# Three rearrangements in the first layer of a fused transformer kernel: a shift matrix through device memory, state matrices on another queue, half units in other places

## The chip, the cores and the metric

The kernel runs on one core of one Trainium2 chip. The metric is the device time of one execution in microseconds (us); lower is better. Engines are called by the names of the profile: PE (TensorE matmul), PEld (its weight loads), DVE (VectorE), ACT (ScalarE), POOL (GpSimd) and SP (SyncE, which issues most transfers). An engine with a q behind it (SPq, ACTq) is the instruction queue that issues DMAs.

## The reference, cut to what matters

Everything is float32, with batch 1, 256 positions and width 1024. The program is one even layer, a feed-forward network, one odd layer, a feed-forward network, and then a second block (feed-forward, mixer, cross attention to a memory, feed-forward, final norm). The change lies in the even layer alone:

```
hn = rmsnorm(x, even_norm)
q, k, v, u = split(hn @ even_w_in, [512, 640, 768])     # 8 query heads, 2 key heads, u has 512 channels
q, k = rmsnorm(q, q_norm), rmsnorm(k, k_norm)            # by head
o_attn = swa_sink_attention(q, k, v, sinks)              # window 128
o_ssm  = s5_mixer(u, a, b, c, d, log_dt, w_glu, b_glu)   # 32 groups, 64 complex states, 16 channels
x = x + concat(o_attn, o_ssm) @ even_w_out
hn = rmsnorm(x, ffn_norm); x = x + (silu(hn @ w_gate) * (hn @ w_up)) @ w_down
```

The state-space mixer `s5_mixer` is a linear recurrence in 64 complex states for each of 32 groups of 16 channels. The kernel computes it in chunks of S = 8 positions: inside a chunk as a product with a block-triangular matrix, and between chunks as a scan over 32 chunk states.

## The kernel before, in words

**Units.** Weights arrive from device memory in units of 1 MB in a ring of three buffers `raw`. SP issues each load (`load`, L563) when the unit that had the buffer is used up (`w_used`). In the even layer units u0 to u0+4 are the five 256-column parts of `even_w_in`: u0 and u0+1 give u transposed (`whole_t`, L712, 16 products each, all in float32), u0+2 to u0+4 give q, k and v (`whole_n`, L724, which can be done in two halves, one for each 128 rows). Unit u0+5 is the gate matrix (L1161), u0+6 and u0+7 multiply the gated mixer output (`out_glu`, L1181), u0+8 and u0+9 the attention output (`out_heads`, L694, split in high and low parts, which ACT makes at L1632 and DVE at L2172). The next unit belongs to the cross attention's memory (`mem_k1`), and then the first feed-forward network begins.

**PE's order** is written out by hand in `even()` (L957). It is: flips (transposes) of the state matrices' raw form `a_raw`; the flips of the normed input, `norm(0)` (L805, the line of all flips); 64 small flips that bring B and C from `bc_nat` into PSUM; u0; u0+1; flips of u into chunks; u0+2; again such flips; flips of the chunked u and of V (`v_in`); the 32 chunk-state products (L1021); the first half of u0+3; the flips of these states, straight and with halves swapped (L805, L1037); the lag products K (L1050), which need B and C scaled by powers (`bb_ready`, `wc_ready`, from a long row of DVE operations that ends at L2483); the second half of u0+3 and the first of u0+4; two products with `jt`; the second half of u0+4; flips of q; `convolve(0)`, the flips of the keys, `convolve(1)` (L1086, L1089); the attention scores (`window_scores`, L1121 to L1130); flips of y; the gate; the output units, with `probs` and `values_t` between them; `out_heads(0)`, `norm(8)` (the flips of the normed memory), `out_heads(1)`.

**The shift.** The lag products K end in SBUF as `lags`: 64 rows (16 channels of each of 4 group columns), 8 lags, 8 groups, 16 channels. For `convolve` they must stand as a block Toeplitz matrix `m_in`, in which the block rows j = 0 to 7 hold the first j+1 lags, shifted. 32 DMAs from SBUF to SBUF do this, one for each j and group column, 18 of them issued by SP and 14 by ACT:

```
for j, cc in M_SP:
    sp.dma_start(m_in[PC * j:PC * j + PC, cc, S - 1 - j:, :, :],
                 lags[32 * cc:32 * cc + PC, 0:j + 1, :, :]).then_inc(m_in_done, 16)
sp.wait_ge(m_in_done, 16 * 4 * S)
```

ACT issues its share (L1847) between its copies `qkv_out(1)` and `qkv_out(2)` (L1808, L1811); the latter empties unit u0+4 for the norm of q and k (squares on ACT L1851, a sum on DVE L2511, a root on POOL L1583 to L1585, the product on DVE L2518). POOL adds the skip term to lag 0 first (L1578).

**Start.** SP issues x, three small loads for a and dt (`ssm_loads`, L551), the constants, the gain, two loads of B and four of C (`bc_loads`, L620), and then u0 to u0+2 and 19 small vectors (L624). ACT has no load of its own there.

**The end of the layer.** DVE takes the softmax rows in a fixed order: `front` (maximum, L2536 to L2540) and `back` (division, L2376 to L2378) for six tiles, and `gated` (L2549), the product that `out_glu` waits for. After `norm(8)` ACT makes the high parts (L1693) and DVE the low parts (L2217) of the normed memory, then DVE adds the layer's output to x (L2341).

## Time and profile before

| what | value |
|---|---|
| median of 3 runs | 1213.48 us (1212.47 to 1213.51) |
| the profiled execution: its time / its span | 1212.6 us / 1210.9 us |
| PE busy in the span | 1182.2 us (98%) |
| DVE / ACT / POOL busy | 782.9 / 588.2 / 64.9 us |
| bytes moved | 206.05 MB, mean 170 GB/s |
| even layer: start of the first unit / of the scores / of `out_glu` | 16.84 / 84.09 / 98.03 us |
| start of the unit `mem_k1`, behind the even layer's last unit | 131.98 us |

The span runs from the first to the last instruction of the profile; times inside it are counted from its start. "Idle before, releaser" is what ended an engine's wait. A line number is one of the kernel before. One product of float32 operands is two records of PE, a flip is one record.

### The profile page before, as it was taken

The numbers are of one execution on the slowest core, as the hardware profiler recorded it, in microseconds if no ns is written. First come the engines' busy times: TensorE is split into PE (matmuls) and PEld (weight loads), VectorE is DVE, ScalarE is ACT, GpSimd is POOL, SyncE is SP. The second block draws the span as 40 slices with busy tenths as digits, with TensorE's granted clock in tenths as the row PEclk, the third lists the DMA queues.
The fourth block names the chain that finished last, engine by engine and source line by source line (L and its number), as shares of the span: only waits on it lengthen the run. The fifth ranks groups of instructions, "written<-read, shape, count | busy, mean of one in ns | idle before, by whom it ended". The sixth has DMA issues, their size and how long they took to land.

```text
span 1210.9 us, 17637 instructions
## 1 busy us (share of the span) xinstructions
PE 1182.2 (98%) x7043; PEld 1021.8 (84%) x7043; DVE 782.9 (65%) x845; ACT 588.2 (49%) x729; POOL 64.9 (5%) x81
## 2 busy tenths in 40 slices
PE   6989999999999999999999999999999999999997
PEld 5866888888899988888888888888889988888886
DVE  6956666666755557666667666667594646766665
ACT  5446644444566655434445444345574545444443
POOL 2110000000002110000000000000011000000000
PEclk9999999999999999999999999999999999999999
DMA  8254565565544346555655656555533534656561
GB/s 208 88 144 135 165 189 194 182 199 182 184 156 150 130 153 195 189 194 183 198 179 171 201 180 207 176 199 174 182 128 117 181 132 131 199 183 199 180 201 70
DMA packets 158120, 206.05 MB, mean 170 GB/s; under 512 B 9833, under 2 KB 131249, under 8 KB 158065
## 3 DMA queue, kind: packets, MB, share of 16 engines
q1 hardware_dynamic: 157616, 204.51, 52.6%
q10 hardware_dynamic: 448, 0.77, 0.4%
q8 instruction: 39, 0.64, 0.2%
q14 instruction: 17, 0.13, 0.0%
HBM read 203.04 MB, written 1.05 MB: 169 GB/s over the span
## 4 chain that ended last, share of the span: by engine, by line
PE 90%; DVE 5%; ACT 2%; DMA 1%; ACTq 1%; issue 1%; SPq 1%; POOL 0%; POOLq 0%; DVEq 0%
PE outp L753 26%; PE acc L694 20%; PE outp L694 19%; PE outp L757 13%; PE acc L805 2%; PE outp L712 1%; PE outp L724 1%; PE outp L1181 1%; DVE w_lo L2172 1%; DVE h_pair L2217 1%; PE outp L859 1%; DMA raw<-in_even_w_in_dram 1%; ACTq L1847 1%; ACT w_hi L1632 0%; ACT h_pair L1693 0%
## 5 line engine op out<-in xcount | busy, mean ns | idle before, releaser
L1632 ACT ACTIVATE w_hi<-raw 128x2048 fp32r<-128x2048 f32 x177 | 339.5, 1918 | 411.5 <-PE outp L757 283.7
L2172 DVE TENSOR_TENSOR w_lo<-raw,w_hi 128x2048 fp32r<-128x2048 f32 x177 | 405.4, 2290 | 177.5 <-ACT w_hi L1632 177.4
L753 PE MATMUL outp<-h_pair,w_hi 128*128 128x512 f32 x1056 | 253.8, 391 | 0.3
L753 PEld LDWEIGHTS outp<-h_pair,w_hi 128*128 128x128 f32 x1056 | 195.0, 188 | 42.6 <-DVE h_pair L2217 4.2
L757 PEld LDWEIGHTS outp<-h_pair,w_lo 128*128 128x128 f32 x1056 | 135.4, 191 | 5.1
L694 PE MATMUL acc<-w_hi,f_lo 128*128 128x512 f32 x352 | 137.4, 390 | 0.0
L694 PE MATMUL acc<-w_hi,f_hi 128*128 128x512 f32 x352 | 137.4, 390 | 0.0
L694 PE MATMUL acc<-w_lo,f_hi 128*128 128x512 f32 x352 | 137.0, 389 | 0.0
L757 PE MATMUL outp<-h_pair,w_lo 128*128 128x256 f32 x1056 | 137.0, 283 | 0.0
L694 PE MATMUL outp<-w_hi,h_pair 128*128 128x512 f32 (+1 forms) x416 | 114.0, 361 | 0.5 <-DVE w_lo L2172 0.3
L2271 DVE TENSOR_REDUCE arena<-outp 128x256 f32<-128x512 f32 x88 | 56.7, 687 | 58.4 <-PE outp L757 56.1
L2284 DVE TENSOR_REDUCE arena<-outp 128x256 f32<-128x512 f32 x88 | 56.7, 687 | 56.3 <-PE outp L757 56.1
L694 PEld LDWEIGHTS outp<-w_hi,h_pair 128*128 128x128 f32 x416 | 73.0, 189 | 13.8 <-issue 1.6
L694 PEld LDWEIGHTS acc<-w_lo,f_hi 128*128 128x128 f32 x352 | 66.1, 188 | 14.0
L694 PEld LDWEIGHTS acc<-w_hi,f_hi 128*128 128x128 f32 x352 | 66.2, 188 | 12.6
L753 PE MATMUL outp<-m_pair,w_hi 128*128 128x512 f32 x320 | 76.7, 392 | 0.0
L694 PEld LDWEIGHTS acc<-w_hi,f_lo 128*128 128x128 f32 x352 | 66.2, 188 | 12.3
L694 PE MATMUL outp<-w_lo,h_pair 128*128 128x512 f32 (+1 forms) x208 | 74.2, 357 | 0.0
L694 PE MATMUL outp<-h_pair,w_hi 128*128 128x256 f32 x384 | 70.8, 286 | 0.0
L753 PEld LDWEIGHTS outp<-m_pair,w_hi 128*128 128x128 f32 x320 | 59.3, 188 | 12.5 <-issue 0.2
L694 PEld LDWEIGHTS outp<-h_pair,w_hi 128*128 128x128 f32 x384 | 59.8, 191 | 0.9 <-issue 0.5
L1553 POOL TENSOR_SCALAR arena<-arena 128x1 f32<-128x1 f32 x20 | 9.7, 487 | 911.0 <-ACT xn L1655 887.4
(334 smaller groups left out, 1427.0 us busy)
## 6 DMA issues: line engine op xcount, KB each, us to landing
raw<-in_ffn_w_gate_dram SPq DMA_DIRECT2D x44, 1024.0 KB, 5.6
raw<-in_ffn_w_up_dram SPq DMA_DIRECT2D x44, 1024.0 KB, 5.5
raw<-in_ffn_w_down_dram SPq DMA_DIRECT2D x44, 1024.0 KB, 4.9
raw<-in_odd_w_in_dram SPq DMA_DIRECT2D x12, 1024.0 KB, 5.2
raw<-in_w_in_dram SPq DMA_DIRECT2D x10, 1024.0 KB, 5.2
raw<-in_even_w_in_dram SPq DMA_DIRECT2D x5, 1024.0 KB, 9.1
raw<-in_even_w_out_dram SPq DMA_DIRECT2D x4, 1024.0 KB, 6.9
raw<-in_cross_wk_dram SPq DMA_DIRECT2D x4, 1024.0 KB, 5.7
```

Source lines behind the costliest of these rows:

```text
L694: ins = nc.tensor.matmul(dst, lhs, rhs, start=start and n == 0, stop=stop_ and n == 2, skip_group_check=skip)
L712: ins = nc.tensor.matmul(outp[:, k % NB, m * L:(m + 1) * L], w[:, c, m * P:(m + 1) * P], h_f32[:, c, :], start=c == 0, stop=c == C - 1)
L724: ins = nc.tensor.matmul(outp[:, k % NB, t * UW:(t + 1) * UW], h_f32[:, c, t * P:(t + 1) * P], w[:, c, :], start=c == 0, stop=c == C - 1)
L753: nc.tensor.matmul(bank, w[0][:, c, m * P:(m + 1) * P], x[:, :, c, :], start=c == 0, stop=c == C - 1, skip_group_check=True)
L757: ins = nc.tensor.matmul(outp[:, (k + m) % NB, 0:L], w[1][:, c, m * P:(m + 1) * P], x[:, 0, c, :], start=False, stop=c == C - 1, skip_grou ...
L805: return nc.tensor.transpose(dst, src, ident[base:base + rows, base:base + rows])
L859: nc.tensor.matmul(outp[:, (k + m) % NB, :].rearrange("p (a l) -> p a l", l=L)[:, :, rows], w[:, c, m * P:(m + 1) * P], m_pair[:, :, c, ro ...
L1181: ins = nc.tensor.matmul(outp[:, (ko + 2 * j + t) % NB, :], sig[:, c, t * P:(t + 1) * P], w[:, c, :], start=c == 0, stop=False, skip_group ...
L1632: A(w_hi[:, slot(u), :], raw[:, u % RAW, :], ACT.Copy).then_inc(w_hi_ready, 1)
L2172: tt(w_lo[:, slot(u), :], raw[:, u % RAW, :], w_hi[:, slot(u), :].bitcast(F32), ALU.subtract).then_inc(w_lo_ready, 1)
L2271: V.reduce_sum(silu[:, j % 2, m * L:(m + 1) * L], bank.rearrange("p (a l) -> p l a", l=L), AX).then_inc(out_free[(k + m) % NB], 1)
L2284: V.reduce_sum(b[:, m * L:(m + 1) * L], bank.rearrange("p (a l) -> p l a", l=L), AX).then_inc(out_free[(k + m) % NB], 1)
```

## The change

Five edits, all in the even layer:

1. The three loads for a and dt, the two of B and the loads of C go from SP's queue to the front of ACT's. C is loaded in its natural order in two loads instead of four.
2. The flips of B (32) stay ahead of u0; those of C go between u0 and u0+1, as 64 products with the identity, 32 rows by 64 columns each, since C's halves are now made by writing the product twice, to partitions 0 to 63 and 64 to 127. DVE waits for the first, ACT for both before its copies L1788.
3. The first half of u0+3 moves from behind the chunk-state products to ahead of the flips of the chunked u; the second half moves from behind the lag products K to ahead of them.
4. The shift goes through a device-memory tensor `lag_rows`: four DMAs write the lags (two by SP, two by ACT), both queues wait for all four, and eight DMAs (one for each j, all group columns together) read them into `m_in`, four on each queue. SP then loads u0+6 and u0+7 ahead of the memory `mem_sb`. ACT's `qkv_out(1)` comes before its copies of the lags.
5. PE does `convolve(1)` right after `convolve(0)`, then the flips of the keys, then those of y, then the scores. ACT loads its table for the gelu before it copies the keys. DVE does `gated(0)` ahead of the first two divisions. `norm(8)` stands ahead of `out_heads(0)`.

```diff
+        b_loads = [(bc_nat[G * j:G * j + G, :].rearrange("g (h m) -> g h m", h=2),
+                    a[n][0].rearrange("g n p -> g (n p)").unsqueeze(1).to_broadcast([G, 2, 1024]))
+                    for j, n in enumerate(["ssm_b_re", "ssm_b_im"])]
-        bc_loads += [(bc_nat[G * j + 64:G * j + 64 + G, :].rearrange("g (p h n) -> g p h n", h=2, n=N)[:, :, h, :],
-                      a[n][0]) for j, n in enumerate(["ssm_c_re", "ssm_c_im"]) for h in range(2)]
+        c_loads = [(bc_nat[G * j + 64:G * j + 64 + G, 0:N * PC], a[n][0].rearrange("g p n -> g (p n)"))
+                   for j, n in enumerate(["ssm_c_re", "ssm_c_im"])]
+        lag_rows = nc.dram_tensor("lag_rows", (4 * PC, S * 8 * PC), F32, kind="Internal").ap()
+        def lags_out(eng, cc):
+            eng.dma_start(lag_rows[PC * cc:PC * cc + PC, :],
+                          lags[32 * cc:32 * cc + PC, :, :, :].rearrange("p s i c -> p (s i c)")).then_inc(lag_out, 16)
+        def lags_in(eng, j):
+            eng.dma_start(m_in[PC * j:PC * j + PC, :, S - 1 - j:, :, :].rearrange("p a s i c -> p a (s i c)"),
+                          lag_rows.rearrange("(a p) m -> p a m", p=PC)[:, :, 0:(j + 1) * 8 * PC]).then_inc(m_in_done, 16)
...
@@ SP @@
-                for j, cc in M_SP:
-                    sp.dma_start(m_in[PC * j:PC * j + PC, cc, S - 1 - j:, :, :],
-                                 lags[32 * cc:32 * cc + PC, 0:j + 1, :, :]).then_inc(m_in_done, 16)
-                sp.wait_ge(m_in_done, 16 * 4 * S)
+                for cc in range(2):
+                    lags_out(sp, cc)
+                sp.wait_ge(lag_out, 16 * 4)
+                for j in (7, 5, 3, 1):
+                    lags_in(sp, j)
+                sp.wait_ge(m_in_done, 16 * S)
+                for j in range(2):
+                    load(u0 + 6 + j, quarter(w_out, 1, j), 512)
                 sp.dma_start(mem_sb, a["mem_2"][0].rearrange("(t p) f -> p t f", p=P)).then_inc(mem_in, 16)
...
@@ PE @@
+                pe.wait_ge(b_in, 16 * 2)
                 for p in range(PC):
-                    for j in range(4):
...
+                    for j in range(2):
+                        ins = flip(outp[:, (OUT["even_b"] + j) % NB, p * G:(p + 1) * G],
+                                   bc_nat[G * j:G * j + G, p::PC], G, G * j)
                 ins.then_inc(bc_flipped, 1)
+                whole_t(u0, OUT["even_u0"], fresh=chunks(0))
+                pe.wait_ge(c_in, 16 * 2)
...
+                for p in range(PC):
+                    for h in range(2):
+                        for j in range(2):
+                            rows = slice(G * (j + 2), G * (j + 3))
+                            ins = nc.tensor.matmul(outp[N * h:N * h + N, (OUT["even_c"] + j) % NB, p * G:(p + 1) * G],
+                                                   bc_nat[rows, p * N:(p + 1) * N], ident[rows, rows],
+                                                   start=True, stop=True)
+                ins.then_inc(bc_flipped, 1)
+                whole_t(u0 + 1, OUT["even_u1"])
...
                 u_chunked(1)
+                whole_n(u0 + 3, k0 + 3, (0,))
...
-                whole_n(u0 + 3, k0 + 3, (0,))
                 emptied(pe, ACC["st"], 2)
...
+                whole_n(u0 + 3, k0 + 3, (1,))
                 pe.wait_ge(bb_ready, 2)
                 pe.wait_ge(wc_ready, 1)
...
-                whole_n(u0 + 3, k0 + 3, (1,))
                 whole_n(u0 + 4, k0 + 4, (0,))
...
                 convolve(0)
-                (flips of the keys)
                 convolve(1)
-                (window_scores(0), then the flips of y)
+                (flips of the keys, the flips of y, then window_scores(0))
...
+                norm(8)
                 out_heads(0, True)
-                norm(8)
                 out_heads(1)
...
@@ ACT @@
+                (the loads ssm_loads, b_loads, c_loads ahead of everything)
+                qkv_out(1)
                 (copies of the lags)
-                qkv_out(1)
-                for j, cc in M_ACT: (14 DMAs)
+                for cc in (2, 3):
+                    lags_out(nc.scalar, cc)
+                act.wait_ge(lag_out, 16 * 4)
+                for j in (6, 4, 2, 0):
+                    lags_in(nc.scalar, j)
                 qkv_out(2)
...
-                qk_out(ACC["kt"], k_t, L, 1)
                 y_out(1)
                 nc.scalar.preload_act_table_set("gelu_apprx_tanh_and_others")
+                qk_out(ACC["kt"], k_t, L, 1)
...
@@ DVE @@
+                gated(0)
                 back(0)
                 back(1)
-                gated(0)
-                back(2)
                 gated(1)
```

Lines in round brackets stand for lines that are only moved.

## Rows read from the trace of the kernel before

**Rows 1.** The page: the span, and the chain that ended last by engine.

```profile
span 1210.9 us, 17637 instructions
...
PE 90%; DVE 5%; ACT 2%; DMA 1%; ACTq 1%; issue 1%; SPq 1%; POOL 0%; POOLq 0%; DVEq 0%
```

**Rows 2.** Windows by stage: length, busy PE, PEld, DVE, ACT, POOL, clock, DMA.

```profile
33.31:61.18 27.87, 24.56 (x248) 22.02 (x247) 27.32 (x17) 13.75 (x27) 2.14 (x2) 1.00 0.24 77
61.18:84.09 22.91, 19.73 (x255) 16.14 (x255) 11.97 (x13) 5.99 (x10) 5.31 (x4) 1.00 0.47 117
```

**Rows 3.** The chain, 0 to 35: start, duration, what.

```profile
7.38 9.07 DMA raw<-in_even_w_in_dram
...
16.84 16.47 PE outp L712 x64
```

**Rows 4.** Timeline 0 to 20: start, duration, operation, idle before and its releaser.

```profile
6.08 0.63 ACT L1655 ACTIVATE xn<-x_sb 128x512 f32<-128x512 f32 x1 [4.00 <-DMA x_sb<-in_x_dram]
...
9.40 3.87 PE L805 MATMUL acc<-arena,xn 128*128 128x128 f32 x16 [1.30 <-DVE xn L2206]
...
13.62 1.97 PE L805 MATMUL outp<-arena 32*128 32x32 f32 x64 [0.35 <-DMA arena<-in_ssm_c_im_dram]
```

**Rows 5.** Window of one microsecond, columns as in rows 2.

```profile
3.00:4.00 1.00, 0.00 (x0) 0.00 (x0) 0.00 (x0) 0.00 (x0) 1.00 (x1) 1.00 0.97 401
```

**Rows 6.** Windows of the products L712 alone: length, PE, PEld, clock, DMA share, GB/s.

```profile
17.00:21.20 4.20, 4.20 (x10) 3.35 (x11) 1.00 1.11 351
22.00:26.20 4.20, 4.20 (x21) 3.71 (x20) 1.00 0.31 38
```

**Rows 7.** Groups by form, 44 to 64: busy us, mean ns, idle before.

```profile
L805 PE MATMUL acc<-arena 32*128 32x32 f32 x32 | 2.1, 221 | 1.1 <-ACT arena L1800 1.1
...
L1037 PE MATMUL acc<-arena 128*64 128x128 f32 x32 | 2.0, 276 | 0.0
```

**Rows 8.** Timeline 53 to 64, columns as in rows 4.

```profile
53.87 0.60 ACT L1953 ACTIVATE arena<-acc 128x512 f32<-128x512 f32 x1 [0.27 <-PE acc L1021]
...
61.18 2.06 PE L1050 MATMUL acc<-arena 128*16 128x128 f32 x64 [0.95 <-issue]
```

**Rows 9.** The shift's issues by SP: ns of one, first and last start.

```profile
L632 SPq DMA_DIRECT2D arena_end<-arena x18: 589/596/763, 65.2 to 76.3; - x18
```

**Rows 10.** DMA issues: size of one, median us from issue to landing.

```profile
arena_end<-arena ACTq DMA_DIRECT2D x4, 64.0 KB, 2.7
...
out_dram<-xn SPq DMA_DIRECT2D x2, 512.0 KB, 2.7
```

**Rows 11.** Window of the shift, columns as in rows 2.

```profile
70.00:80.00 10.00, 7.88 (x78) 5.92 (x80) 4.17 (x5) 3.03 (x4) 0.32 (x2) 1.00 0.60 103
```

**Rows 12.** Timeline 60 to 120, columns as in rows 4.

```profile
75.99 0.60 ACT L1811 ACTIVATE arena<-outp 128x512 f32<-128x512 f32 x1 [8.40 <-PE outp L724]
...
78.71 0.43 PE L1086 MATMUL acc<-arena_end,arena 128*32 128x128 f32 x8 [0.79 <-DMA arena_end<-arena]
...
84.81 1.28 ACT L1870 ACT_TABLE_LOAD   x1
...
98.03 2.38 PE L1181 MATMUL outp<-raw,arena 128*128 128x512 f32 x5 [0.98 <-DVE arena L2549]
...
118.05 0.69 DVE L2382 TENSOR_TENSOR h_pair<-acc,h_pair 128x512 fp32r<-128x512 f32 x1 [0.61 <-ACT h_pair L1958]
```

**Rows 13.** The chain, 60 to 90.

```profile
63.24 3.67 PE outp L724 x16
...
81.76 0.41 PE acc L805 x2
...
84.09 0.67 PE outp L1121 x2
```

**Rows 14.** The chain, 95 to 140.

```profile
117.59 5.70 PE outp L694 x24
...
129.72 2.20 DVE w_lo L2172
```

More of the change, by code:

```diff
@@ L138, in build @@
                  if (what == "half" and i % 2 == 0) or (what == "values" and i < 6)]
-    OUT = plan([("even_bc", 4), ("even", 5), ("even_sc", 4), ("even_out", 4), ("mem_k1", 1), ("ffn0", 44), ("mem_k0", 1), ("odd", len(ODD_BANKS)),
+    OUT = plan([("even_b", 2), ("even_u0", 1), ("even_c", 2), ("even_u1", 1), ("even", 3), ("even_sc", 4), ("even_out", 4), ("mem_k1", 1), ("ffn0", 44), ("mem_k0", 1), ("odd", len(ODD_BANKS)),
                 ("odd_out", 4), ("mem_k2", 1), ("ffn1", 44), ("mem_k3", 1), ("ffn2", 44), ("mem_v0", 1), ("mix", 10),
@@ L548, in _ @@
             sp.dma_start(x_sb[:, :, :], a["x"][0].rearrange("(t p) f -> p t f", p=P)).then_inc(x_loaded, 16)
-            if "even" in running:
-                for dst, src in ssm_loads:
-                    sp.dma_start(dst, src).then_inc(ssm_in, 16)
             sp.dma_start(early, a["consts"][:, 0:EARLY_W]).then_inc(consts_in, 16)
@@ L618, in _ @@
                 w = by_p(a["even_w_in"][0])
-                for dst, src in bc_loads:
-                    sp.dma_start(dst, src).then_inc(bc_in, 16)
                 for j, n in enumerate([3, 4, 0]):
@@ L957, in even @@
             def even():
-                u0, k0 = UNITS["even"], OUT["even"]
+                u0, k0 = UNITS["even"], OUT["even"] - 2
                 pe.wait_ge(consts_in, 16)
@@ L1092, in even @@
                 convolve(0)
-                k = ACC["kt"]
-                acc_taken(pe, k)
-                pe.wait_ge(qk_ready, 1)
-                for t in range(T):
-                    ins = flip(acc[:, k % NB, t * P:(t + 1) * P], qkv[:, t, 512:640])
-                ins.then_inc(acc_ready, 1)
                 convolve(1)
@@ L1133, in window_scores @@
                                 ins.then_inc(sc_ready if i < 2 else acc_ready, 1)
-                emptied(pe, ACC["qk"], 2)
-                emptied(pe, ACC["kt"])
-                pe.wait_ge(mask_ready, 1)
-                window_scores(0)
+                k = ACC["kt"]
+                acc_taken(pe, k)
+                pe.wait_ge(qk_ready, 1)
+                for t in range(T):
+                    ins = flip(acc[:, k % NB, t * P:(t + 1) * P], qkv[:, t, 512:640])
+                ins.then_inc(acc_ready, 1)
                 for j in range(2):
@@ L1763, in even @@
             def even():
-                u0, k0 = UNITS["even"], OUT["even"]
+                u0, k0 = UNITS["even"], OUT["even"] - 2
+                for dst, src in ssm_loads:
+                    nc.scalar.dma_start(dst, src).then_inc(ssm_in, 16)
+                for dst, src in b_loads:
+                    nc.scalar.dma_start(dst, src).then_inc(b_in, 16)
+                for dst, src in c_loads:
+                    nc.scalar.dma_start(dst, src).then_inc(c_in, 16)
                 act.wait_ge(x_loaded, 16)
@@ L1784, in even @@
                 A(small[:, 15, :], turns[:, 1, :], ACT.Sin, scale=TWO_PI).then_inc(lam_sin, 1)
-                act.wait_ge(bc_flipped, 1)
-                for j, part in ((2, cr), (3, ci)):
-                    k = OUT["even_bc"] + j
+                act.wait_ge(bc_flipped, 2)
+                for j, part in ((0, cr), (1, ci)):
+                    k = OUT["even_c"] + j
                     A(part.rearrange("p g c -> p c g"), outp[:, k % NB, :].rearrange("p (c g) -> p c g", g=G),
@@ L1842, in even @@
                       ACT.Copy).then_inc(acc_free[k % NB], 1)
-                qkv_out(1)
                 act.wait_ge(kz_ready, 1)
                 act.wait_ge(k_ready, 1)
-                for j, cc in M_ACT:
-                    nc.scalar.dma_start(m_in[PC * j:PC * j + PC, cc, S - 1 - j:, :, :],
-                                        lags[32 * cc:32 * cc + PC, 0:j + 1, :, :]).then_inc(m_in_done, 16)
+                for cc in (2, 3):
[3 more added lines that the diff above has]
+                    lags_in(nc.scalar, j)
                 qkv_out(2)
@@ L2398, in even @@
             def even():
-                u0, k0 = UNITS["even"], OUT["even"]
+                u0, k0 = UNITS["even"], OUT["even"] - 2
                 dve.wait_ge(x_loaded, 16)
@@ L2556, in even @@
                     front(nth)
+                gated(0)
                 back(0)
                 back(1)
-                gated(0)
-                back(2)
                 gated(1)
-                for nth in range(3, 6):
+                for nth in range(2, 6):
                     back(nth)
```

43 lines of the change are left out of this document (20 added, 23 removed), and 2 rows, old and new, of the table ACC.

## The prediction

> **What bounds the kernel now.** I read the page first, for its chain: PE carries 90% of what ended last, in a span of 1210.9 us [rows 1]. So outside the even layer nothing is to be had here, and a microsecond saved on PE's way through the layer is kept. Then the windows by stage, to see where PE is not full. Between 33.31 and 61.18 PE is busy 24.56 of 27.87 us and DVE 27.32: there DVE's row of operations for B and C (it ends with `wc_ready`) runs beside PE without a pause, and both arrive at the lag products K together, PE with 0.95 us of waiting [rows 2, 8]. Between 61.18 and 84.09 PE is busy 19.73 of 22.91 us [rows 2]. Then the chain and the timeline of the start: x lands at 6.08, PE flips x until 13.27, does 64 small flips from 13.62 to 15.59, and begins u0 at 16.84, when its weights, asked for at 7.38, have landed after 9.07 us [rows 3, 4]. Last the shift: SP alone issues 18 DMAs at 0.6 us each from 65.2 on, `convolve(0)` starts at 78.71 behind them, and ACT comes to `qkv_out(2)` only at 75.99, behind its own 14 issues [rows 9, 12].
>
> **Start.** Seven loads on ACT at about 0.5 us each cost ACT 3.5 us, inside the 4.00 us that it waits for x anyway [rows 4]. SP asks for u0 after three loads instead of twelve, some 5 us earlier, so its wait of 9.07 us ends long before PE is free; that wait goes. What is late next is PE itself. x used to have the DMA engines to itself at 401 GB/s [rows 5]; now 512 KB of B are under way beside its second half. Between 0 (they start too late to matter) and 512 KB / 401 GB/s = 1.3 us, plus 0.3 for the small ones: x lands 0 to 1.6 us later; I take 0.8, the middle. This moves all that hangs on x. The Trainium skill (DMA: Bandwidth & Descriptors, "Issuing engines are not separate DMA queues") says that the two queues share the same 16 engines and take turns, which speaks against the edit: by it nearly all of B's bytes would go ahead of x's end, the 1.6 us end; by the row of 401 GB/s and a late start, the 0.
>
> The flips of B are 32 of 64. The 64 ran at 0.031 us, taking turns over four groups of 32 partitions [rows 4]; 32 flips from one group took 2.1 us, 0.065 each [rows 7]. With two groups the price lies between 32 x 0.031 = 1.0 and the full 2.0; I take 1.5. So u0 starts at 13.27 + 0.8 + 1.5 + 0.1 = 15.7, **1.15 us earlier**.
>
> In u0 PE makes 10 records in 4.2 us, later 21 in as long, though the granted clock reads 1.00 in both windows [rows 6]: half and full pace, 1.2 and 2.4 GHz. It is slow from 16.84 until about 21.6, which costs 2.4 us. The sum keeps this loss; ends 0 and -2.4.
>
> **C between u0 and u0+1.** 64 float32 products are 128 records. Nearest rows: 0.031 us per flip when all groups take turns, and 2.0 / 32 = 0.062 per record for the products with the identity L1037, which alternate between two column halves as these do but move 128 columns, not 32 [rows 4, 7]. So 3.9 us, or 7.9; below, half of 3.9, if they pair up over rows and columns, is 2.0. I take 3.5: the columns are few, so what is left is the pace of issue. Half of the old 64 flips was C's, but it lay ahead of u0 and is counted there. **+3.5.** ACT's copies of B and C's parts have time until DVE needs them at 44.
>
> **The halves of u0+3.** Ahead of the chunked flips the first half covers ACT's copies, for which PE waited 1.1 us [rows 7]: -1.1. It no longer covers the copies of the chunk states (0.60 us; the last begins at 53.87, with the half [rows 8], and the handovers add 0.3): +0.9. The second half, ahead of K, takes the wait for `wc_ready`: -0.95 [rows 8]. PE ends u0+4 at 75.5 - 1.15 + 3.5 - 1.15 = 76.7, 1.2 late. But K is late by that and by the half of 3.65 us: it ends at 63.24 + 4.85 = 68.1 [rows 8, 13], and the lags, with ACT's copy and POOL's addition (63.24 to 65.2 before), are ready at 70.0 instead of 65.2.
>
> **The shift.** Out: two issues per queue; the last, issued 0.6 later, lands after 2.15 (64 KB within SBUF took 2.7, 512 KB into device memory also 2.7, of which 512 KB / 401 GB/s = 1.3 is the bytes' own time: 1.6 to 2.7 for 64 KB, the middle taken [rows 5, 10]): 2.75. The Trainium skill (DMA: Bandwidth & Descriptors, "Anatomy of one DMA") puts most of a transfer's fixed 2 us to the receipt of the write and calls device memory the heaviest target; the store row shows no such surcharge, and the sum has none. Back in: four issues of 0.64 on each queue, the last landing 2.7 behind its start: 4.6 at least; 1.18 MB at 300 GB/s takes 3.9 and starts 1.4 behind the first issue: 5.25. The old shift moved 103 GB/s at a share of 0.60 [rows 11], or 172 at full share: 6.9 + 1.4 = 8.3 at most. So `m_in` is whole at 70.0 + 2.75 + 5.25 = **78.0** (77.3 to 81.1), against 78.7 [rows 12]. The 13.5 us of the old shift shrink to 8.0, and 4.85 of the 5.5 gained are spent ahead of it. ACT leaves its queue at about 75.3, ahead of u0+4's end at 76.7; nobody waits there. The DMA traffic that u0+6 and u0+7 now precede (`mem_sb`, needed at 102) costs nothing.
>
> **To the scores.** Two convolutions of 1.9 (82.17 to 84.09 was one [rows 13]) end at 81.9. Behind them ACT copies y1 (0.6), loads its table (1.28 [rows 12]), copies the keys (0.5), with three handovers of 0.15: scores at **84.7**. By the other way, u0+4's end at 76.7 plus 5.8 (75.99 to 81.6, and 0.2) has the keys normed at 82.5, in time. So +0.6 against 84.09 [rows 13]. Flips of y and scores change places; DVE's two `front` rows decide the gate's start either way, 5.7 us behind.
>
> **The end.** PE waited 0.98 us for `gated(0)` at 98.03 [rows 12]; behind the last `front` instead of behind two divisions it is done 2 us earlier: **-0.98**. `norm(8)` ahead of `out_heads(0)`: its last bank is free only when DVE has made the low parts, at 118.74 [rows 12], so PE ends it at 120.1 and starts the heads 2.5 us later than at 117.59; without the 1.9 us of flips between them, both take 2 x 5.7 [rows 14] and end at 131.2 instead of 130.5. But the memory's parts and DVE's split, behind which `mem_k1` began at 131.98 [rows 14], are now early: it starts at 131.2, -0.8, and 0.15 more for the row flips behind it. **-0.95.**
>
> **Sum.** +0.6 - 0.98 - 0.95 = -1.3 us. The profiled execution took 1212.6 for its span of 1210.9, and stands 0.9 below the median of 1213.48. 1212.6 - 1.3 = 1211.3 by its own time, **1212.2** by the median. Less than 0.2% (2.43 us) is about what a measurement of this kernel cannot tell from no change.
>
> **Rivals.**
> - *Faster, by the clock.* PE's pause of 1.25 us ahead of u0 goes [rows 4]. If full pace comes at u0's start instead of 4.8 us into it, 2.4 us go with it, and since PE bounds everything up to the scores all of it arrives: 1209.8. For it: PE is now busy without a break from 10 on. Against: it was busy from 9.40 to 15.59 too, with a break of 0.35, and began u0 slow. The Trainium skill (TensorE: Matmul & The Clock Gate, Part 1) says that sustained busyness raises the clock; by it a part or all of the 2.4 us could go.
> - *Slower, by C's products.* At 0.062 us a record they take 7.9 instead of 3.5: K, the shift and the scores slip by 4.4, to 1216.6. It decides beyond 3.5 + 3.7 = 7.2 us. Against: a quarter of the columns.
> - *The shift is no faster than before.* At 8.3 us for the way in, the scores start 3.1 later: 1215.3, slower.
> - *x is on time and the small prices are at their low ends:* -0.8 for x, -0.5 for B, up to -1.5 for C: 1209.4.
>
> **Chances.** The forecast, with its neighbours within 0.2%: 0.48; its own range is 1211.1 to 1214.5. Clock 0.26 and low ends 0.10: faster 0.36. C's products 0.08, the shift 0.08: slower 0.16. The range leaves a tenth on each side: below, it takes in the clock's and the low ends' times, 1209.2; above, the late shift, 1215.4.
>
> **What the profile will show.** u0 (L712 of before) at 15.7 and without a DMA as releaser; 128 records of C in 3.5 us; K's end near 68; the lag DMAs from 70.0, `m_in` read at 78; no wait ahead of `out_glu` and of `mem_k1`. I am wrong if x lands at 7.7 or on time, if u0 takes under 8.5 us (it took 9.5), if C takes over 5, if K ends outside 66 to 70, or if the way in lasts over 7 us.

## The result: slower by 0.26%, and the profile after

The changed kernel takes 1216.52 us (median of 19 runs, 1214.39 to 1219.92) against 1213.48 (19 runs): ratio 1.0026, 95% interval 1.002 to 1.0032. The forecast was 1212.2 with a range that ended at 1215.4. It is outside, on the other side.

The profiled execution of the changed kernel took 1219.92 us, the longest of its 19. Its stages show where time goes, but not in the amounts of the median, so sizes are read below from medians of experiments too.

The page: the span, and the chain by engine, beside [rows 1].

```profile
span 1218.2 us, 17808 instructions
...
PE 92%; DVE 3%; DMA 2%; ACT 2%; issue 0%; ACTq 0%; SPq 0%; POOL 0%; POOLq 0%
```

The timeline of PE and ACT in the first 30 us, beside [rows 4]; below it the piece of the chain that stands where [rows 3] had 9.07 us of the same transfer.

```profile
6.25 0.63 ACT L1672 ACTIVATE xn<-x_sb 128x512 f32<-128x512 f32 x1 [0.25 <-DMA x_sb<-in_x_dram]
...
13.06 1.95 PE L813 MATMUL outp<-arena 32*128 32x32 f32 x32
15.72 8.86 PE L720 MATMUL outp<-h_whole,raw 128*128 128x256 f32 x32 [0.71 <-DMA raw<-in_even_w_in_dram]
24.51 2.07 PE L989 MATMUL outp<-arena 32*64 32x32 f32 x128
26.50 7.17 PE L720 MATMUL outp<-h_whole,raw 128*128 128x256 f32 x32
```

```profile
2.27 13.41 DMA raw<-in_even_w_in_dram
```

u0 begins at 15.72, as forecast, but not for the forecast's reason: PE waits 0.71 us for the weights, whose load takes 13.41 us instead of 9.07, with x, B and C under way beside it, and lands only at 15.67. C's products take 2.07 us. PE ends u0+1 at 33.68 in the chain, 0.37 behind the 33.31 of [rows 2].

The timeline of PE and ACT's queue in the middle of the layer, beside [rows 8, 12]:

```profile
54.59 1.95 PE L1040 MATMUL acc<-arena 128*32 128x128 f32 x64 [1.30 <-ACT arena L1978]
...
60.18 3.72 PE L732 MATMUL outp<-raw,h_whole 128*128 128x256 f32 x16
63.83 2.02 PE L1069 MATMUL acc<-arena 128*16 128x128 f32 x64
...
67.39 0.84 ACTq L516 DMA_DIRECT2D lag_rows<-arena  x2
71.26 1.80 ACTq L521 DMA_DIRECT2D arena_end<-lag_rows  x4
...
74.51 1.04 PE L813 MATMUL acc<-arena 128*128 128x128 f32 x8
82.03 0.65 PE L1104 MATMUL acc<-arena_end,arena 128*32 128x128 f32 x8 [6.48 <-DMA arena_end<-lag_rows]
...
91.06 1.00 PE L813 MATMUL acc<-arena 32*128 32x32 f32 x29 [1.49 <-ACT arena L1881]
91.99 1.22 PE L1133 MATMUL outp<-h_pair 128*128 128x512 f32 x2
```

K ends at 65.9 instead of 63.24 (the moved half unit stands at 60.18 ahead of it), the lags leave at 67.39 instead of 65.2, the way out takes 3.85 us and the way in 10.7 (14.6 together, where the old shift took 13.5), and PE stands idle for 6.48 us ahead of `convolve`, where it had waited 0.79 [rows 12]. Eight products of `convolve` take 0.65 us instead of 0.43. The scores start at 91.99 (92.06 by the chain) instead of 84.09 [rows 13], and the feed-forward network's start is late with them. The DMA issues of the way in (size, median us to landing), beside [rows 10]:

```profile
arena_end<-lag_rows SPq DMA_DIRECT2D x1, 256.0 KB, 5.1
arena_end<-lag_rows ACTq DMA_DIRECT2D x1, 224.0 KB, 6.2
...
arena_end<-lag_rows ACTq DMA_DIRECT2D x1, 32.0 KB, 9.4
```

Windows, columns as in [rows 2] (the last three are the clock, the DMA share and GB/s), beside [rows 11]:

```profile
76.00:77.00 1.00, 0.00 (x0) 0.00 (x0) 0.27 (x1) 1.00 (x2) 0.00 (x0) 1.00 1.05 132
...
81.00:82.00 1.00, 0.00 (x0) 0.00 (x0) 0.00 (x0) 0.00 (x0) 1.00 (x1) 0.50 0.00 0
82.00:84.00 2.00, 1.97 (x40) 1.82 (x44) 0.00 (x0) 0.00 (x0) 0.60 (x1) 0.50 0.48 32
...
94.00:98.00 4.00, 4.00 (x22) 2.61 (x20) 2.44 (x9) 2.47 (x8) 0.00 (x0) 0.50 0.00 0
```

Two things are to be seen. During the way in the DMA engines are near a full share but move little: 132 GB/s in this window, and over the whole way in 1.18 MB for a summed share of 8.9 us, which is 133 GB/s at a full share (x had 401 [rows 5]). And the granted clock is 0.50 (1.2 instead of 2.4 GHz) from 81 to 87, from within PE's idle 6.48 us on, and again from 92 to 98, behind the wait that ends at 91.06.

The end is as planned. In the chain `out_glu` follows the gate without a wait, and the memory's unit the heads:

```profile
99.98 7.12 PE acc L1178 x32
107.10 6.87 PE outp L1198 x16
...
129.01 13.76 PE outp L702 x72
142.77 0.90 PE acc L813 x8
```

From `out_glu` to the row flips behind `mem_k1` it is 142.77 - 107.10 = 35.67 us. Before, it was 135.24 - 98.03 = 37.21 (this row of its chain was not shown; [rows 12] for the other):

```profile
135.24 1.16 PE acc L805 x8
```

### The profile page after: what moved, and what is told of

Read it like the earlier page. It is cut to its first block, busy times and chain, and to the rows that moved or that the text cites. A ratio compares the mean times of both kernels' runs of the same rounds, so it can differ in the third digit from the quotient of the medians.

```text
span 1218.2 us, 17808 instructions
## 1 busy us (share of the span) xinstructions
PE 1188.4 (98%) x7139; PEld 1027.7 (84%) x7139; DVE 783.2 (64%) x845; ACT 588.2 (48%) x729; POOL 64.6 (5%) x81
## 3 DMA queue, kind: packets, MB, share of 16 engines
q10 hardware_dynamic: 944, 1.49, 0.6%
## 4 chain that ended last, share of the span: by engine, by line
PE 92%; DVE 3%; DMA 2%; ACT 2%; issue 0%; ACTq 0%; SPq 0%; POOL 0%; POOLq 0%
PE outp L761 26%; PE outp L702 20%; PE acc L702 20%; PE outp L765 13%; PE acc L813 2%; PE outp L720 1%; PE outp L732 1%; PE outp L1198 1%; DMA raw<-in_even_w_in_dram 1%; DVE w_lo L2197 1%; DVE h_pair L2242 1%; DMA arena_end<-lag_rows 1%; PE outp L867 1%; PE acc L1178 1%; ACT w_hi L1649 0%; ACT h_pair L1710 0%
## 5 line engine op out<-in xcount | busy, mean ns | idle before, releaser
L702 PEld LDWEIGHTS outp<-w_hi,h_pair 128*128 128x128 f32 x416 | 73.1, 189 | 13.4 <-DVE w_lo L2197 1.3
## 6 DMA issues: line engine op xcount, KB each, us to landing
raw<-in_even_w_in_dram SPq DMA_DIRECT2D x5, 1024.0 KB, 13.4
```

Of the source, the lines that this page charges most:

```text
L702: ins = nc.tensor.matmul(dst, lhs, rhs, start=start and n == 0, stop=stop_ and n == 2, skip_group_check=skip)
```

## The experiments

All ratios are against the kernel before, run on the same chip. Where two experiments are compared by their medians, they may come from two chips, on which the kernel before had 1213.1 to 1213.9 (1212.8 in a single run). "Start", "shift", "halves", "end" are the edits 1 and 2, 4, 3, and 5 without its reordering of keys and flips of y.

### Parts undone in the changed kernel

**The half unit and ACT's copy behind.** The changed kernel with the second half of u0+3 behind K, and `qkv_out(1)` behind ACT's lag transfers.

```diff
-                whole_n(u0 + 3, k0 + 3, (1,))
                 pe.wait_ge(bb_ready, 2)
...
+                whole_n(u0 + 3, k0 + 3, (1,))
                 whole_n(u0 + 4, k0 + 4, (0,))
...
-                qkv_out(1)
...
                     lags_in(nc.scalar, j)
+                qkv_out(1)
                 qkv_out(2)
```

> The changed kernel with one thing put back: the second half of u0+3 stands behind the lag products K again, and ACT's copy of that unit behind its lag DMAs. Theory A (the late K and a slow way in together leave PE idle, and the idle time also costs clock): K ends near 62.7 instead of 65.9, the lags go out at 64, m_in is whole near 79, PE idles about 3 us instead of 6.5 ahead of convolve, the granted clock stays 1.00 there; 3 to 6 us faster than the changed kernel, about 1211 to 1213. Theory B (only the way in counts, K's place does not): m_in near 82 still, no gain.

Measured: 1212.68 us, 0.999 (0.9982 to 0.9999): 3.8 below the changed kernel. Its timeline of PE, and a window:

```profile
61.05 2.04 PE L1068 MATMUL acc<-arena 128*16 128x128 f32 x64 [1.30 <-issue]
...
76.87 0.43 PE L1104 MATMUL acc<-arena_end,arena 128*32 128x128 f32 x8 [0.63 <-DMA arena_end<-lag_rows]
```

```profile
84.00:88.00 4.00, 4.00 (x25) 2.79 (x20) 0.61 (x1) 3.32 (x5) 0.00 (x0) 0.50 0.65 256
```

PE waits 1.30 us ahead of K and only 0.63 ahead of `convolve`, which starts 5.2 us earlier at the full clock. The second stretch at half clock stays. ACT's copy, which was put back too, is not the cause by the trace of the changed kernel: there it ran from 63.94 to 64.6, and ACT then waited for the lag products (0.40 and 0.32 us), so the lags were not late by it. What is left is the half unit. It filled a pause of PE with work and delayed the transfer that everything waits for.

Not all of the 5.2 us is shown to be its effect. The lags leave 2.3 us earlier (65.08); the way out is 1.0 us shorter here (2.8) and the way in 1.8 (8.9), with the same transfers. In the other runs with unchanged rows the way in was 9.9 to 11.4 us; why it was short here is not shown.

**The old shift.** The changed kernel with the 32 transfers within SBUF in the place of the twelve.

> The changed kernel with the old shift (32 DMAs within SBUF, 18 by SP, 14 by ACT), all other edits kept. Theory A: issued from 67.3 on at 0.6 us each, m_in is whole near 80.8, 1.2 us earlier than through device memory, PE still idles 5 us and the clock still falls: within 2 us of the changed kernel, 1214.5 to 1216.5. Rival (the way through device memory is the whole loss): back to 1212 or below.

Measured: 1217.7 us (6 runs), 1.0036 (1.0024 to 1.0048). This is above both expectations, and by the intervals no different from the changed kernel (1.0026). PE waits 5.3 us, `convolve` starts at 78.8, at half clock. That is 3.2 us earlier than in the changed kernel's profile, but most of it arises at the start: in this execution the 32 products of u0 took 7.17 us instead of 8.86, the pace of the full clock from the first one on, and K ends at 63.8 instead of 65.9. From K's end to `convolve` the old shift takes 15.0 us and the new one 16.1, so that the 1.2 us of the expectation are there, and the clock falls behind it as before.

**Spare products in the wait.** Six products with `jt` that nobody reads, ahead of PE's wait for `m_in`.

```diff
+                acc_taken(pe, ACC["y0"])
+                for _ in range(6):
+                    nc.tensor.matmul(acc[:, ACC["y0"] % NB, :], jt,
+                                     g_st[:, 0:16, :].rearrange("p g c -> p (g c)"), start=True, stop=True)
                 pe.wait_ge(m_in_done, 16 * S)
```

> The changed kernel with six more products of 128x512 on PE while it waits for m_in, into the bank that convolve(0) then overwrites; nothing else differs. Theory A (the idle time costs clock, not only itself): m_in still whole near 82, but the granted clock stays 1.00 behind it, convolve takes 3.9 us instead of 6.5, and the scores and the gate run at full pace: 1 to 5 us faster than the changed kernel. Rival (the clock has nothing to do with the idle time, or the slow stretch falls elsewhere): no gain, and a granted clock near 0.5 at 82 to 88 as before.

Measured: 1214.49 us (11 runs), 1.0011 (1.0002 to 1.0019): 2.0 below the changed kernel. Its timeline:

```profile
74.81 5.32 PE L1094 MATMUL acc<-arena 128*128 128x512 f32 x12
81.52 0.42 PE L1108 MATMUL acc<-arena_end,arena 128*32 128x128 f32 x8 [1.40 <-DMA arena_end<-lag_rows]
```

`m_in` is no earlier, PE only works more, and the kernel is faster: eight products take 0.42 us again and the clock reads 1.00 in every window from 76 to 98. So the clock's fall was about 2 us of the median (1.8 by the ratios, whose intervals just do not meet).

### Parts done alone in the kernel before

**The shift alone.**

> The kernel before with the new shift alone (four DMAs out, eight in, PE and all other orders as before). Lags ready at 65.2, but ACT's two writes wait for the unit behind K, as its old issues did (67.0); writes land at 69.7, and with a way in of 7.3 to 9.4 us, as in the runs so far, m_in is whole at 77.5 to 79.5 against 78.7. Theory A (the new shift by itself neither gains nor loses; it lost because it began late): 1212.5 to 1214. Rival (the way through device memory is itself the loss): 1215 or more.

Measured: 1213.85 us, 1.0002 (0.9993 to 1.0011). The last landing of the way in came 8.6 us after its issue. `m_in` is whole at 79.7 instead of 78.7: PE waits 2.08 us, and `convolve` begins at half clock (0.65 us for eight products). So the new shift is no faster than the old one even where it starts in time:

```profile
79.73 0.65 PE L1098 MATMUL acc<-arena_end,arena 128*32 128x128 f32 x8 [2.08 <-DMA arena_end<-lag_rows]
```

**The start alone.**

> The kernel before with the start alone: loads for a, dt, B and C on ACT's queue, C's flips as 128 short products between u0 and u0+1. Theory A: u0 starts at 15.7 instead of 16.8, C takes 2.1 us, u0+1 ends within 0.5 us of before: 1212.5 to 1214, no change. Rival (a stolen 0.3 us of x and a slower DMA of the first units matter): 1215 or more.

Measured: 1216.42 us, 1.0021 (1.0012 to 1.003). This missed. u0 starts at 16.54, u0+1 ends at 34.45, which is 1.15 behind before; the other part arises between 44 and 56. Timeline and window of this run:

```profile
45.96 8.98 PE L812 MATMUL acc<-arena 32*128 32x32 f32 x64 [1.10 <-ACT arena L1823]
55.87 1.95 PE L1038 MATMUL acc<-arena 128*32 128x128 f32 x64 [0.94 <-ACT arena L1976]
```

```profile
47.00:54.00 7.00, 7.00 (x44) 6.94 (x43) 6.86 (x5) 4.18 (x7) 0.00 (x0) 0.51 0.10 38
```

The flips took 5.79 us before, behind the same wait of 1.10 us; here they run at half clock.

**The start with the waits filled.** The start alone, with four spare 128x128 products at each of these two waits.

> The start edit alone, as before, with four spare 128x128 products with the identity ahead of each of the two waits in which PE stood idle 1.1 and 0.9 us there (for the copies of the chunked u, and for those of the flipped V); their result is used by nobody. In the start alone PE's clock was half between 47 and 54, where the 64 small flips took 8.98 us instead of 5.79. Theory, the clock is the greater part of the start's cost: with the waits filled it stays whole, the 64 flips take 5.8 us, the chunk-state products start at 53 to 53.5 instead of 55.87, and the median is 2 to 3 us lower than the start's alone (1216.4), at 1213.3 to 1214.5. Rival, the clock falls for another reason: still 0.50 there, 1216 to 1217.5.

Measured: 1213.13 us (11 runs), 0.9998 (0.9989 to 1.0007), 3.3 below the start alone:

```profile
45.75 5.79 PE L812 MATMUL acc<-arena 32*128 32x32 f32 x64 [0.21 <-ACT arena L1829]
51.37 1.06 PE L1034 MATMUL acc<-arena 128*128 128x128 f32 x8
52.79 1.95 PE L1044 MATMUL acc<-arena 128*32 128x128 f32 x64 [0.36 <-ACT arena L1982]
```

```profile
47.00:54.00 7.00, 6.64 (x100) 6.43 (x102) 6.86 (x5) 5.22 (x11) 0.00 (x0) 1.00 0.10 34
```

Here the 64 flips begin 0.94 us later than before (45.75 against 44.81), but K at 61.18 as before, since PE's wait of 0.95 us ahead of K takes that up; in the start alone K began at 64.18. So, as far as the intervals tell, the start's cost in the median was the clock; without it the edit brings nothing and costs nothing.

**The loads alone on ACT's queue,** with C in its old four loads and all flips ahead of u0.

> The kernel before with nothing but the three loads for a and dt and the six for B and C moved from SP's queue to the front of ACT's; all 64 small flips stay ahead of u0, in their old form. Theory: what the start edit costs is the clock, which in the start alone was half from 47 to 54 us, behind the flips of the chunked u, and 1 us of C's products; with the move alone u0's weights land at 15.7 to 16.5, the flips end at 15.6 to 17, u0 starts at 15.8 to 17, and everything to the scores comes 0 to 1 us earlier unless the clock falls: 1212.3 to 1213.5, and 1215 to 1216 if it falls at 47 to 54 again. Rival, the DMA traffic is itself the cost (B, C and u0 beside x): u0 starts after 17, x or the first flips are late, and 1214 to 1216 with a full clock.

Measured: 1221.52 us (5 runs), 1.0065 (1.0051 to 1.0078): both numbers missed. Its timeline:

```profile
22.57 1.97 PE L800 MATMUL outp<-arena 32*128 32x32 f32 x64 [7.45 <-DMA arena<-in_ssm_c_im_dram]
25.81 16.74 PE L707 MATMUL outp<-h_whole,raw 128*128 128x256 f32 x64 [1.26 <-issue]
```

C's last load, issued from 6.87 on, lands at 22.5, beside the three units of weights. In the start alone, with C in its natural order and its flips behind u0, the same move costs 5 us less (1216.42); the two were not tried apart.

**The end alone, and the start with the end.**

> The kernel before with the end alone: gated(0) ahead of the first two divisions on DVE, norm(8) ahead of out_heads(0) on PE. By the prediction's two terms 0.98 and 0.95 us: 1211.4. Rival (each wait only moves to the next engine): 1213.5, no change.

Measured: 1210.6 us (11 runs), 0.998 (0.9971 to 0.9989): 2.5 gained (1.3 to 3.5 by the interval), more than the 1.9 of the two terms.

> Start and end of the change, with the halves, the shift and the order around convolve as before. If the edits add up: the sum of the two single runs, 1211 to 1212. If the start costs as much as the end gains: 1213.5.

Measured: 1212.49 us, 0.999 (0.9981 to 0.9999): 1.9 above the end alone. The two single results, +3.3 and -2.5, would give 1213.9; in this execution the flips behind the wait of 1.10 us took 7.45 us, not the 8.98 of the start alone.

### Why the way in is slow

**Another source.** The eight transfers read a weight matrix, each its own part; the lags are left out of the convolution.

> The changed kernel with the way in reading, for each block row j, 64 rows of its own in a weight tensor instead of lag_rows; sizes, queues, order and destinations are the same. It leaves the lags out of the convolution. Theory S (all eight reads want the same 256 KB just written): the way in takes 5 to 6 us instead of 9.4. Theory D (sixteen partitions per DMA, one per DMA engine, is what is slow): it takes 9 us again, near 125 GB/s.

Measured: 1215.73 us (10 runs), 1.002 (1.0007 to 1.0033), landing 4.9 to 10.1 us after the issue, 11.4 us for the whole way in at 137 GB/s per full share. The source is not it.

**Rows spread by eight partitions.** `m_in[PC * j:PC * j + PC, ...]` becomes `m_in[j::S, ...]`.

> The changed kernel, with the way in written to other partitions: block row j goes to partitions j, j+8, ..., 120 + j instead of 16j to 16j+15. Source, sizes, order and queues are the same. What it leaves out: the lags stand in the wrong rows, so the convolution is of other numbers. In the changed kernel the eight transfers landed 5.1 to 9.4 us after their issue, at a full share of the DMA engines and only 110 to 190 GB/s, and another source did not change that. Theory D, sixteen neighbouring partitions reach few ports of SBUF: spread over all 128 partitions the way in (first issue to last landing, 10.8 us in the changed kernel) takes 5 to 6 us, the rate at a full share rises over 250 GB/s, PE waits 1 to 3 us instead of 6.5 ahead of the convolution, the clock does not fall there, and the median is 3 to 5 us below that of the changed kernel: 1211.5 to 1213.5. Rival, the number or the length of the descriptors (16 rows by 4 pieces each): way in still 9 to 10.8 us, 1215.5 to 1217.5.

Measured: 1215.08 us (10 runs), 1.0011 (1.0001 to 1.002). Landings and one window of this run:

```profile
arena_end<-lag_rows SPq DMA_DIRECT2D x1, 256.0 KB, 3.6
...
arena_end<-lag_rows ACTq DMA_DIRECT2D x1, 32.0 KB, 5.8
```

```profile
76.00:77.00 1.00, 0.62 (x6) 0.38 (x4) 0.00 (x0) 0.89 (x2) 0.00 (x0) 1.00 1.03 200
```

The way in shrinks from 10.7 us to 8.0 (72.62 to 80.57), its rate rises to 200 to 230 GB/s. That is half the effect that was expected and between the two numbers of the expectation, and the clock still falls in the wait of 4.0 us.

**One long piece for each row** instead of four, in neighbouring rows and in spread ones.

> The changed kernel, in which each of the eight transfers of the way in moves, for each of its 16 rows, one piece of 2 KB times (j+1) instead of four pieces of 512 B times (j+1); rows, bytes, order and queues are the same. What it leaves out: the lags stand at wrong places. Spreading the rows over the partitions took the way in from 10.8 to 8.0 us and the rate at a full share from some 130 to 230 GB/s, not to the 350 of the weights, so something else is left. Theory, the number or shortness of the pieces: the way in is 1.5 to 3 us shorter than 10.8 here. Rival, only the sixteen partitions count: 10 to 11 us and 110 to 140 GB/s at a full share as before.

> As the run with long pieces, and the rows go to partitions j, j+8, ... 120+j as well; the same is left out. If both count, the way in is 5 to 6.5 us from the first issue to the last landing, four issues of 0.64 us included, and the rate at a full share over 280 GB/s. If only the partitions count: 8.0 us, as with the spread rows alone.

Measured, one run each: 1221.36 us with the last landing 9.6 us after its issue; 1211.91 us with 5.6. The landings are those with short pieces (9.4 and 5.8), and the whole way in is 11.0 and 7.7 us (10.7 and 8.0): number and length of the pieces make no difference that these runs show. The 9 us between the two times are not the transfer's alone. In the second one PE waited 3.52 us ahead of `convolve`, and the clock did not fall there.

**Rows of 8, neighbouring or apart by four.** Each transfer is cut in two of 8 rows.

> The changed kernel, with each of the eight transfers of the way in cut into two of 8 rows: SP moves rows 16j to 16j+7 and ACT rows 16j+8 to 16j+15, for j from 7 down to 0. This is the control of the next run: the same sixteen transfers in the same order. Theory of the ports (a transfer is bound by how many groups of partitions it reaches): two transfers of the same j are under way at a time, all within sixteen neighbouring partitions, so the rate at a full share is 110 to 150 GB/s and the way in 9 to 12 us. Rival, cutting itself helps: under 8 us.

> The same sixteen transfers with the eight rows of each written four partitions apart: partitions 64h + 32(j/4) + j mod 4 + 4k for k from 0 to 7, SP with h = 0 and ACT with h = 1, so that the two together touch all 128 partitions' groups. What it leaves out: the lags stand in the wrong rows. Spreading by eight partitions gave some 200 to 230 GB/s at a full share, not the 350 of the weights. Theory of the ports: with the rows apart by four in both halves the rate is 280 to 400 GB/s in the first microseconds, after which the issues (eight of 0.4 to 0.6 us on each queue, 3.5 to 5 us) bound it; the way in is 5.5 to 7 us. Rival, small transfers from these rows have another bound: 200 to 230 GB/s and 8 us or more, or no better than the control.

Measured, one run each: 1223.63 us with a way in of 71.24 to 85.54 = 14.3 us, and 1215.53 with 71.81 to 80.79 = 9.0. One window of either, first neighbouring, then apart:

```profile
77.00:78.00 1.00, 0.00 (x0) 0.00 (x0) 1.00 (x1) 1.00 (x2) 0.00 (x0) 1.00 0.56 65
```

```profile
77.00:78.00 1.00, 0.00 (x0) 0.00 (x0) 0.00 (x0) 0.00 (x0) 0.00 (x0) 1.00 0.51 198
```

Both expectations missed in us, because transfers of 8 rows keep only half of the DMA engines busy (share 0.4 to 0.6), which neither theory had. With the rows apart the issues are longer too: eight on ACT's queue take 6.2 us instead of 3.1, so the last one ends at 78.03. But the bytes moved per busy engine can be compared. Each way in moves 1.18 MB; the shares of its one-microsecond windows, summed, give the rate at a full share:

| rows of one transfer | run | sum of shares, us | GB/s at a full share |
|---|---|---|---|
| 16 neighbouring | the changed kernel | 8.9 | 133 |
| 8 neighbouring | the control | 6.4 | 184 |
| 16, eight apart | spread rows; with long pieces | 5.5; 5.2 | 214; 228 |
| 8, four apart | the last run | 3.3 | 356 |

Single windows differ more: the neighbouring 8 rows moved 53 to 90 GB/s in the five windows from 75 on (65 at 0.56 is 116 at a full share), those apart 154 to 203 (198 at 0.51 is 388). With source, sizes and order alike, the partitions alone nearly double the rate. They are the largest cause that the runs show, and not the only one: the 16 neighbouring rows moved 133 to 146 in seven runs and 166 in the first experiment, where nothing of the transfers was changed. No run had rows four apart at a full share, so how short the way in can get was not shown.

The Trainium skill (SBUF — State Buffer, "Door 1: The DMA port swizzle") says that a transfer's rate depends on how many of 16 ports its partitions reach; by its table sixteen neighbouring partitions reach 4, those eight apart 8, and those four apart, by two transfers in both halves, all 16. At its 27.2 GB/s for each port that would be 109, 218 and 435. The rows agree in order, and in size with the second (214); the first and the control are above the 109 of four ports (133, 184), and the last is below its bound (356). By the same table two transfers of neighbouring rows with successive j reach 8 ports together, which would allow more than 109; how many are under way at once, no run here shows.

### A version without the start edit

**Shift, end, first half of u0+3 ahead, second behind K, `qkv_out(1)` behind the transfers;** start and order of keys as before.

> The kernel before with the new shift, the first half of u0+3 ahead of the flips of the chunked u, its second half left behind K, ACT's copy of unit u0+3 moved behind ACT's lag transfers, and the edit of the end; the start, the order of keys, flips of y and scores as before. If the parts add up: the end alone gave -2.5, the shift alone 0.0; K no longer has the half unit ahead, the copy no longer delays the lags or the transfers (another 0.6 us), so -2.5 to -3.5: 1209.7 to 1210.7. Rival: the wait ahead of the convolution is over 1.5 us and the clock falls there or at 48 to 54, and it is no better than the end alone: 1210.5 to 1212.5.

Measured: 1210.43 us (6 runs), 0.997 (0.9958 to 0.9983). Its timeline and window:

```profile
78.74 0.43 PE L1098 MATMUL acc<-arena_end,arena 128*32 128x128 f32 x8 [0.99 <-DMA arena_end<-lag_rows]
```

```profile
80.00:84.00 4.00, 4.00 (x94) 3.29 (x90) 0.49 (x2) 1.08 (x2) 3.72 (x2) 0.68 0.85 337
```

It beats both kernels, but is not told apart from the end alone (1210.6) by the intervals: there is 1.78 us of waiting ahead of K and again a fall of the clock in `convolve`.

This trace also shows a part of edit 5 that no experiment took by itself, the order around `convolve`. In the new order PE stands idle for 1.49 us ahead of the flips of y, behind ACT's table load and its copy of the keys, and in the first experiment the clock fell behind that. From the start of `convolve` to `out_glu` it took 22.4 us there (76.87 to 99.25), and 18.6 with the old order here (78.74 to 97.37), although here it is `convolve` that ran slow. Where the clock stayed whole it was 19.7 in the new order (spare products in the wait) and 18.2 in the old one (the end alone). So the new order costs some 1.5 us, and up to 4 with the clock's fall behind its wait:

```profile
83.19 0.94 PE acc L813 x29
...
99.25 6.87 PE outp L1198 x16
```

```profile
97.37 7.03 PE L1193 MATMUL outp<-raw,arena 128*128 128x512 f32 x16
```

(The first two lines are of the chain of the first experiment, the last of the timeline of this version.)

**The same with spare products at three waits.**

> The version without the start edit (measured 1210.43), with spare products at the waits that stand ahead of its slow stretch: 3 ahead of the flips of q, 5 ahead of the wait for the shift, 4 ahead of the chunk-state products. There PE waited 0.89 and 0.99 us from 75.8 on, the clock's mean was 0.90 and 0.68 in the windows 76 to 80 and 80 to 84, and half the products of the first convolution took twice as long. Theory of the clock: the clock stays whole, the first convolution takes 1.9 instead of 3.2 us; but the second waits for the norm of q and k, which ends at about 81.7 in any case, so only 0.3 to 0.8 us of it arrive: 1209.6 to 1210.2. Rival, spare products only add work: 1210.4 to 1211.5.

Measured: 1210.09 us (6 runs), 0.9967 (0.9955 to 0.9979), the lowest, and no different from the last by its interval. The clock stays whole where the wait was filled, and falls at K (0.50 from 61 to 64), behind a wait that was not:

```profile
60.84 3.52 PE L1065 MATMUL acc<-arena 128*16 128x128 f32 x64 [2.17 <-issue]
...
80.12 0.43 PE L1107 MATMUL acc<-arena_end,arena 128*32 128x128 f32 x8 [0.41 <-DMA arena_end<-lag_rows]
```

## Why the prediction was wrong

The step that failed is the shift's way in, "5.25 (4.6 to 8.3)": it took 10.7 us (8.9 to 11.4 in the runs with the same rows). Behind it stood a cost that the sum had at nothing, the fall of PE's clock in the wait.

- **u0 at 15.7: the number held, the reason did not.** x was 0.17 late, not 0.8; B's flips took 1.95, the bound, not 1.5; what is late next is u0's weights (15.67 here, 16.5 in the start alone), not PE. The forecast took the 9.07 us of a load that had the engines nearly to itself; beside B and C it took 13.4 to 14.2.
- **C at 3.5: mis-sized.** 2.07 us for 128 records, 0.016 each, the low bound. PE leaves u0+1 0.37 late; the forecast had 2.35. The other 0.5 is the pace of u0 and u0+1 (8.86 and 7.11 instead of 16.47 together), that is the clock, which the forecast had left as it was.
- **The halves: direction right.** K ends 2.7 late (65.9); the forecast had 4.85, and the 2.0 by which PE left u0+1 earlier than forecast is nearly all of the difference. The forecast saw that the second half delays the lags and counted its 3.65 us as spent against a gain in the shift. The gain was not there, so the loss stood bare: 3.8 us of the median by the first experiment, part of the clock's fall included.
- **The way out at 2.75: 3.85.** The last of the four writes landed 3.45 us after its issue, where the forecast took 2.15, the middle of its bounds, and no surcharge for device memory; in the other runs it was 2.2 to 3.8. The section that the forecast draws on there (the Trainium skill, DMA: Bandwidth & Descriptors, "Anatomy of one DMA") is headed as one on the path of GpSimd's transfers, and these are SP's and ACT's. Whether the 1.3 us more are the surcharge that it speaks of, no run separates.
- **The way in at 5.25: 10.7**, outside its bounds. The forecast took 300 GB/s, somewhat less than x's 401, though x is written to all 128 partitions, and for the upper bound a rate of the old shift scaled to a full share (172 GB/s). Eight large transfers, each into sixteen neighbouring partitions, have 133. The row of 103 GB/s at 0.60 [rows 11] said how slow such rows are, and it was read as an effect of small size.
- **`m_in` at 78.0: 82.0. Scores at 84.7: 91.99** in the profile. `convolve` took 6.5 us instead of 3.8, and the scores behind it ran at half clock too. No step of the forecast had a price for PE's idling beyond the idle time itself. The rival "faster, by the clock" looked at the clock's rise at the start alone; a fall behind a wait in the middle was no case, though it costs 2 us here and 3.3 in the start alone. The last 0.6 to 0.7 us ahead of the scores are the new order's: from the end of `convolve` to the scores it is 3.5 us (88.56 to 92.06), the forecast had 2.8, and had nothing for a clock that falls there. In the kernel before no wait in this stretch was followed by such a fall.
- **The end at -0.98 - 0.95 = -1.9: right, a little small.** 37.21 - 35.67 = 1.5 for the second part, 2.5 in the median for both. One sum of it is wrong: 120.1 + 2 x 5.7 is 131.5, not 131.2, which would have made the second part -0.65.
- **Rivals.** "Slower, the shift is no faster" (1215.3, 0.08) was nearest: right mechanism, with a price that stopped at 8.3 us for the way in. "Slower by C's products" did not occur. Of the low ends x and C came nearly as that rival had them, and brought nothing, since u0 waited for its weights. The clock's early rise did not occur in this profile, but it exists: in two of the other runs with the start edit (the old shift, the other source) u0's 32 products took 7.17 us instead of 8.86. What it is worth in the median is not known.

Put together from medians: the end -2.5; the halves ahead of the lags +3.8; the start 0 to +3.3 as the clock falls or not; the shift alone 0. The sum of 1.3 to 4.6 holds the 3.0 measured, but that is a wide range, and the new order around `convolve` is in it only as far as it is in the +3.8. How the clock's part is split between these in the median execution stays open, since only one execution of each kernel is profiled.

## What to carry to other kernels

Filling an engine's wait is a gain only if nothing on the longest chain stands behind the filler: a transfer's source (here the lags) goes first, and the filler into the time of the transfer. Count as part of a wait's price what the clock does behind it, and look whether independent or even spare products can stand in it. Before sizing a transfer by a rate, compare its partitions and rows with those of the row the rate comes from.

## What the runs showed that was not expected

- The granted clock falls to half behind waits that look harmless: behind 6.48 us of idling, but also in flips behind 1.10 us (start alone, 47 to 54), in `convolve` behind 2.08 (shift alone), in K behind 2.17. The same wait of 1.10 us in the kernel before was not followed by a fall, nor were 3.52 us ahead of `convolve` with long pieces in spread rows: the length of the wait alone does not tell. Spare products in the waits went with a clock of 1.00 there and took 2.0 and 3.3 us off the median.
- Transfers of 16 neighbouring rows moved 110 to 190 GB/s with the DMA engines near a full share; with transfers of 8 rows about half of the engines' time was busy (0.56 and 0.51 in the windows shown). A full share does not tell the rate.
- 128 records of 32 rows by 32 columns with 64-column weights took 2.07 us, 0.016 each; 32 flips of the same rows 1.95, 0.061 each.
- x with 512 KB of B on another queue beside it landed 0.17 us later.
